# A decoder step on one core: two more idle products in the router, another order in the first pair of experts, and the sample rows first at the end

## The reference

```python
h = x + W_o( sigmoid(g_a) * Mamba2_SSD(n) + sigmoid(g_b) * ShortConv(n) )   # n = RMSNorm(x)
h = h + CrossAttn(RMSNorm(h), mem)                                         # 4 heads over 256 memory tokens
h = h + MoE(RMSNorm(h))
y = RMSNorm(h)

# MoE: 32 experts, top 4 of each token, softmax over the four logits
logits = x @ w_router + b_router;  top_v, top_i = top_k(logits, 4);  gates = softmax(top_v)
# one expert on the tokens that chose it
gu = xb @ w_gate_up[e] + b_gate_up[e];  gate, up = split(gu)
gate = min(gate, 7);  up = clip(up, -7, 7)
ys = ((up + 1) * gate * sigmoid(1.702 * gate)) @ w_down[e] + b_down[e]
out[token] += ys * gate_of_token
```

## Time and profile before

| | |
|---|---|
| median of 3 runs | 1407.49 us (1406.94 to 1408.96) |
| the profiled execution | 1408.71 us, of which the span from first to last instruction 1407.0 us |
| PE busy | 1374.1 us, 98% |
| DVE, ACT, POOL busy | 442.0, 218.2, 33.7 us |
| mean granted PE clock | 0.995 of full |
| moved by DMA | 497.24 MB; SP's queue 478.99 MB |

### The profile page before, as it was taken

One profiled execution on the slowest core, in us unless ns is written; L12 is line 12 of the kernel. 1 busy time (PEld: TensorE's weight loads), 2 busy tenths in 40 slices (PEclk: granted clock), 3 DMA queues, 4 the chain that ended last, 5 costly groups with the idle time before them and its releaser, 6 DMA issues.

```text
span 1407.0 us, 16092 instructions
## 1 busy us (share of the span) xinstructions
PE 1374.1 (98%) x6414; PEld 669.7 (48%) x6414; DVE 442.0 (31%) x905; ACT 218.2 (16%) x404; POOL 33.7 (2%) x60
## 2 busy tenths in 40 slices
PE   9999999999999999999999999999999999999997
PEld 7688887677756633333333333333333332333322
DVE  5634344862461412221211312213113121131213
ACT  2220022052123211100101111011011010110102
POOL 0000002200002000000000000000000000000000
PEclk9999999999999999999999999999999999999999
DMA  7644545975379899999999999999999999999995
GB/s 249 215 154 154 178 143 195 375 267 195 119 284 390 349 400 397 423 428 428 428 429 428 429 428 429 428 429 428 429 428 429 428 429 428 428 429 428 429 425 227
DMA packets 72119, 497.24 MB, mean 353 GB/s; under 512 B 8968, under 2 KB 10664, under 8 KB 47368
## 3 DMA queue, kind: packets, MB, share of 16 engines
q1 hardware_dynamic: 65852, 478.99, 82.8%
q0 software_dynamic: 4816, 15.54, 3.1%
q10 hardware_dynamic: 1412, 2.18, 0.5%
HBM read 488.61 MB, written 8.24 MB: 353 GB/s over the span
## 4 chain that ended last, share of the span: by engine, by line
PE 81%; DMA 15%; SPq 2%; DVE 1%; issue 1%; ACT 1%; DVEq 0%
PE bank L1504 77%; DMA wide<-in_w_gate_up 8%; DMA ring<-in_w_gate_up 6%; PE bank L1515 4%; DMA wdt<-in_w_in 1%; DVE wide L1427 1%; SPq L438 1%; SPq L441 0%; DVE wide L1487 0%; ACT wide L624 0%; ACT L634 0%; ACT L664 0%; ACT wide L615 0%; SPq L480 0%; SPq L428 0%
## 5 line engine op out<-in xcount | busy, mean ns | idle before, releaser
L1504 PE MATMUL bank<-ring,wide 128*64 128x512 f32 (+2 forms) x1696 | 403.3, 595 | 5.5 <-DMA ring<-in_w_gate_up 5.0
L1504 PE MATMUL bank<-wide 128*64 128x512 f32 (+6 forms) x1046 | 289.8, 575 | 11.4 <-DVE wide L1427 6.4
L1504 PE MATMUL bank<-tokT,ring 128*128 128x264 f32 x1152 | 264.1, 387 | 0.0
L1504 PEld LDWEIGHTS bank<-ring,wide 128*64 128x64 f32 (+2 forms) x1696 | 132.5, 140 | 258.1 <-issue 246.6
L1504 PEld LDWEIGHTS bank<-tokT,ring 128*128 128x128 f32 x1152 | 216.8, 190 | 41.1 <-issue 5.6
L1504 PEld LDWEIGHTS bank<-wide 128*64 128x64 f32 (+4 forms) x1046 | 98.4, 153 | 175.4 <-issue 122.7
L615 ACT ACTIVATE wide<-bank 64x512 f32<-64x512 f32 (+2 forms) x103 | 57.6, 560 | 339.0 <-PE bank L1504 218.5
L1451 DVE TENSOR_SCALAR wide<-bank 128x512 f32<-128x512 f32 x32 | 22.1, 692 | 274.1 <-PE bank L1504 274.1
L1504 PE MATMUL bank<-flat,wide 128*64 128x512 f32 (+2 forms) x408 | 92.9, 592 | 0.3 <-ACT wide L615 0.3
L1504 PE MATMUL bank<-conv,wide 128*64 128x512 f32 (+1 forms) x400 | 90.3, 593 | 0.0
L884 ACT ACTIVATE wide<-wide 128x512 f32<-128x512 f32 x32 | 20.2, 630 | 427.5 <-DVE wide L1451 427.5
(11 more groups left out here) (259 smaller groups left out, 737.8 us busy)
## 6 DMA issues: line engine op xcount, KB each, us to landing
ring<-in_w_gate_up SPq DMA_DIRECT2D x64, 2048.0 KB, 26.1
ring<-in_w_down SPq DMA_DIRECT2D x32, 2048.0 KB, 27.4
flat<-in_w_gate_up SPq DMA_DIRECT2D x16, 2048.0 KB, 24.5
conv<-in_w_gate_up SPq DMA_DIRECT2D x16, 2048.0 KB, 26.0
wide<-in_w_gate_up SPq DMA_DIRECT2D x16, 2048.0 KB, 27.4
tokT<-in_w_gate_up SPq DMA_DIRECT2D x16, 2048.0 KB, 25.1
ring<-in_w_in SPq DMA_DIRECT2D x15, 2048.0 KB, 12.4
wide<-in_w_down SPq DMA_DIRECT2D x8, 2048.0 KB, 25.6
```

The lines of the kernel that those rows point to most:

```text
L1504: last[0] = pe.matmul(out, lhsT, rhs, start=start, stop=stop)
```

## The change

1. Router: three `stay_warm` products of 512 columns take the place of one of 512 and one of 128. They stand ahead of `turn_tokens`, between the two experts' hidden biases, and behind `rank`. The products of `total` move from ahead of the first gather to between the two halves of `turn_rows`.
2. First pair: chunk 8 goes to ring place 8, chunk 9 to `acc` and `ytok`. So the refill of chunk 17 waits for stage 9 instead of 10, and ACT's first values of `acc` for stage 10 instead of 9. PE does `down` of the first expert right behind the eight `gate_up` stages; the gather stands behind stage 11, and `turn_rows` behind stage 12. ACT's `copy_rows` and DVE's `spread` move back with them. The other pairs keep their order.
3. End: sample rows first in `last_scatter`, in DVE's sums and in ACT's squares. Their root's reciprocal is DVE's, both multiplications and the store are POOL's. SP stores the prompt rows alone.

```diff
-        FIRST_SLOT = [0, 1, 2, 6, 3, 4, 5, 7, 9, 8, 0, 1]
+        FIRST_SLOT = [0, 1, 2, 6, 3, 4, 5, 7, 8, 9, 0, 1]
...
-            sp.dma_start(acc[:, :, :], moe_chunk(0, 8)[:, 0:3, :]).then_inc(moe_full[9], 16)
-            sp.dma_start(ytok, moe_chunk(0, 8)[:, 3, :]).then_inc(moe_full[9], 16)
+            sp.dma_start(acc[:, :, :], moe_chunk(0, 9)[:, 0:3, :]).then_inc(moe_full[9], 16)
+            sp.dma_start(ytok, moe_chunk(0, 9)[:, 3, :]).then_inc(moe_full[9], 16)
...
-            for g, done_stages in zip(range(AHEAD, AHEAD + 8), (1, 2, 3, 5, 6, 7, 8, 10)):
+            for g, done_stages in zip(range(AHEAD, AHEAD + 8), (1, 2, 3, 5, 6, 7, 8, 9)):
...
-            sp.wait_ge(S["y_ready"], 4)
-            sp.dma_start(outs[1].rearrange("b s n -> (b s) n"), acc[0:TS, 2, :]).then_inc(S["y_out"], 16)
-            sp.wait_ge(S["y_out"], 64)
+            sp.wait_ge(S["y_out"], 48)
...
+            pool.wait_ge(S["gfin_in"], 16)
+            pool.wait_ge(S["s_root"], 1)
+            st(pool.tensor_scalar(acc[0:TS, 2, :], acc[0:TS, 2, :], rfin[0:TS, 2:3], None, ALU.mult))
+            pool.tensor_tensor(out=acc[0:TS, 2, :], in0=acc[0:TS, 2, :], in1=gfin[0:TS, :], op=ALU.mult)\
+                .then_inc(S["s_ready"], 1)
+            pool.wait_ge(S["s_ready"], 1)
+            pool.dma_start(outs[1].rearrange("b s n -> (b s) n"), acc[0:TS, 2, :]).then_inc(S["s_out"], 16)
+            pool.wait_ge(S["s_out"], 16)
...
                 sigmoid(1)
-                if not final:
+                if not (first or final):
                     copy_rows(at(2, 3))
                 copy_turned(1)
                 if first:
-                    s.wait_ge(S["stage_done"], at(12, 9))
+                    s.wait_ge(S["stage_done"], at(12, 10))
...
                 copy_y(0)
+                if first:
+                    copy_rows(at(2, 3))
                 copy_y(1)
...
-            for i, t in enumerate((0, 1, 2)):
+            for i, t in enumerate((2, 0, 1)):
...
-                if not final:
+                if not (first or final):
                     spread(at(2, 2))
                 v.wait_ge(S["gt_full"], at(1, 1))
                 v.tensor_copy(gT, bank[4][:, 0:T]).then_inc(S["gT_ready"], 1)
+                if first:
+                    spread(at(2, 2))
...
+            accumulate(beyond(n), 0, True)
+            v.wait_ge(S["scat_read"], beyond(n)(5, -4))
+            v.memset(small[:, 310:311], 0.0).then_inc(S["tile_done"], 1)
+            accumulate(beyond(n), 1, True)
+            accumulate(beyond(n), 2, True)
+            v.wait_ge(S["scat_read"], beyond(n)(5, -2))
+            v.memset(small[:, 311:312], 0.0).then_inc(S["tile_done"], 1)
+            v.wait_ge(S["f_rms"], 1)
+            v.reciprocal(rfin[0:TS, 2:3], rfin[0:TS, 2:3]).then_inc(S["s_root"], 1)
+            accumulate(beyond(n), 3, True)
+            accumulate(beyond(n), 4, True)
+            v.wait_ge(S["scat_read"], beyond(n)(5, 0))
+            v.memset(small[:, 312:313], 0.0).then_inc(S["tile_done"], 1)
+            finish(1)
             finish(2)
...
             route(KB - 1)
+            stay_warm(bank[1], 512)
             turn_tokens(KB - 2)
             turn_tokens(KB - 1)
...
-            stay_warm(bank[1], 512)
-            for name, k in (("xo", 6), ("rs", 0), ("rt", 2), ("xtok", 3)):
+            for name, k in (("xo", 6), ("rs", 0)):
                 emptied(pe, name, k)
             pe.wait_ge(S["crossed_in"], 96)
-            hidden_bias(first_pair, 0)
+            hidden_bias(first_pair, 0, (0,))
+            emptied(pe, "rt", 2)
+            stay_warm(bank[7], 512)
+            emptied(pe, "xtok", 3)
+            hidden_bias(first_pair, 0, (1,))
...
+            stay_warm(bank[7], 512)
+            emptied(pe, "xtok", 5)
+            pe.wait_ge(S["xtok_ready"], 3)
+            gather(1)
+            turn_rows(1, (0,))
             b = free_bank(pe, "total")
...
-            stay_warm(bank[4], 128)
-            pe.wait_ge(S["xtok_ready"], 3)
-            gather(1)
-            turn_rows(1)
+            turn_rows(1, (1,))
...
+                elif first:
+                    output_bias(buf)
+                    down(0)
+                    turn_acts(1)
+                    turn_gates()
+                    down(1, (0,))
+                    pe.wait_ge(S["gT_ready"], at(1, 1))
+                    gather(at(1, 2))
+                    down(1, (1,))
+                    turn_rows(at(2, 3))
```

More of the change, by code:

```diff
@@ L1421, in accumulate @@
             def accumulate(at, j, last=False):
-                v.wait_ge(S["scat_full"], at(5, (j - 1) % 5 - 4 if last else j - 4))
+                v.wait_ge(S["scat_full"], at(5, j - 4))
                 if j == 0:
@@ L2009, in gather, with turn_rows @@
                     last[0].then_inc(S["xy_full"], 1)
-            def turn_rows(count):
-                for h in range(2):
+            def turn_rows(count, halves=(0, 1)):
+                for h in halves:
                     pe.wait_ge(S["xgt_ready"], count + h)
@@ L2037, in last_scatter @@
                 pe.wait_ge(S["gT_ready"], at(1, 0))
+                for h in range(2):
+                    mm(bank[5][32 * h:32 * h + TS, :], gT[:, TP:T], ytok[:, 512 * h:512 * h + 512])
+                last[0].then_inc(S["scat_full"], 1)
                 for t in range(2):
@@ L2041, in last_scatter, with hidden_bias @@
                         last[0].then_inc(S["scat_full"], 1)
-                for h in range(2):
-                    mm(bank[5][32 * h:32 * h + TS, :], gT[:, TP:T], ytok[:, 512 * h:512 * h + 512])
-                last[0].then_inc(S["scat_full"], 1)
-            def hidden_bias(at, buf):
+            def hidden_bias(at, buf, experts=(0, 1)):
                 pe.wait_ge(S["onehot_ready"], at(1, 1))
-                for e in range(2):
+                for e in experts:
                     for b in range(2):
@@ L2117, in turn_acts, with down @@
                     last[0].then_inc(S["turned"], 1)
-                def down(e):
+                def down(e, parts=(0, 1)):
                     pe.wait_ge(S["actT_ready"], at(2, e + 1))
-                    for part in range(2):
+                    for part in parts:
                         w = landed(8 + 2 * e + part)
@@ L2130, in down, with turn_gates @@
                         last[0].then_inc(S["stage_done"], 1)
+                def turn_gates():
+                    pe.wait_ge(S["selg_ready"], at(1, 1))
+                    for t, (c, r) in enumerate(TILES):
+                        turn(bank[4][:, c:c + r], selG[0:r, t, :])
+                    last[0].then_inc(S["gt_full"], 1)
                 if not first:
@@ L2159, in experts @@
                     pe.wait_ge(S["xg_ready"], at(2, 3))
-                pe.wait_ge(S["selg_ready"], at(1, 1))
-                for t, (c, r) in enumerate(TILES):
-                    turn(bank[4][:, c:c + r], selG[0:r, t, :])
-                last[0].then_inc(S["gt_full"], 1)
-                down(1)
+                    turn_gates()
+                    down(1)
             experts(first_pair, 0, 0, first=True)
```

22 lines of the change are left out of this document (8 added, 14 removed).

## The result

The changed kernel takes 1413.14 us (median of 9 runs, 1409.89 to 1415.26) against 1406.94 us for the kernel before, run beside it (9 runs, 1403.85 to 1408.96): ratio 1.0035, 95% interval 1.0022 to 1.0047. It is slower by 0.2 to 0.5%; the forecast said 1402.6 us, and its range ended at 1406.3. The profiled span is 1411.7 us against 1407.0.

A forecast was written before the change was run, and what follows sets the result against it. PE's pace bounds the kernel until 1007 us, then the weight stream. Router and first pair -4.8, end -0.7, sum -5.5: 1403.2 as profiled, 1402.0 from the median, middle taken 1402.6 us; range 1400.4 to 1406.3.

The forecast's parts named there:

- The end, forecast -0.7: Behind the last weights: samples first and POOL's share of the work end the span 0.7 us earlier, near SP's row.
- it ends between 1404.3 and 1410.0: End: POOL's two products, issue and store finish in this span of us, giving -0.9 to +3.0 against 1407.0.
- SP's path, forecast -0.9: End: SP's last prompt store issued at 1403.5 to 1403.7 instead of 1404.81, less 0.2 for its size: -0.9 us.
- Rival (3): End: POOL finishes at its upper bound, +3.0 instead of -0.7; all -1.8, 1406.3 us; chance 0.06.
- Rival (4): End: POOL's store sets it and takes 14.1 us; +10.1, with the -4.8 +5.3, 1413 us; chance 0.04.
- DVE's last multiplication: End: POOL's two-input product may block it, losing up to 1.4 us, +0.5 instead of -0.7; counted in the range only.
- I give back 0.2: End: allowance of 0.2 us because SP's last store is 256 KB instead of 32 KB.
- Router, forecast -2.7: Router: with the clock held, `gate_up` starts at 483.0 instead of 485.6; -2.7 us, bounds -3.2 and +0.5.
- rival (1): Router: the granted clock falls all the same; -1.7, with the end -2.4, 1405.7 us; chance 0.22.
- the idle product between the biases can hold `rank` by some tenths: Router: this delays `rank`, and so `select`, by some tenths of a us; gather taken to start at 476.5.
- First pair, forecast -2.1: First pair: earlier refill requests shrink the weight stream's hole from 4.7 to 2.6 us; -2.1 us.
- Later requests follow every 3.5 us, so no third hole appears: Weight stream behind the eleventh refill: requests come faster than the 4.90 us a chunk takes, so no further idle stretch.

The follow-up runs named there:

- e5: The kernel before with the new end alone, but SP issues the sample store and POOL still multiplies; ratio 1.0011 (0.9999 to 1.0023).
- e6: As e5, but POOL takes its two-input product with the gain first and the one-input scaling last; ratio to before 1.0001 (0.9990 to 1.0011).
- e1: The kernel before with the router's part of the change alone; ratio 1.0001 (0.9989 to 1.0014).
- e7: The kernel before with idle products where PE waits in the router, biases kept together, `total` between the transposes' halves; ratio 0.9987 (0.9974 to 0.9999).
- e2: The kernel before with the first pair's new order alone; ratio 0.9998 (0.9986 to 1.0010).
- e8: The kernel before with the first pair's new order in every pair but the last; ratio 0.9991 (0.9979 to 1.0003).
- e13: The kernel before, but POOL issues the sample store at the end and SP waits for it; ratio 1.0024 (1.0013 to 1.0035).
- e11: The kernel before, but POOL issues the sample store at the end and waits for it itself; ratio 1.0028 (1.0014 to 1.0042).

## Why the prediction was wrong

*The end, forecast -0.7, measured +4.2.* The step that failed was where POOL ends: "it ends between 1404.3 and 1410.0", made of two products, an issue and a store. Those terms were nearly sound. The products took 2.85 and 2.33 us (bounds 1.4 to 2.3 each, so one is over), the issue 0.60, the landing 2.9 (bounds 2.2 to 6.0), and POOL's wait was over at 1407.8, or 1407.3 in the time of before. That is 0.7 later than SP's wait was over before, within the range of -0.9 to +3.0. Missing was a term behind the last one: POOL's DRAIN of 3.50 us, which before lay at 461.76 us, where nothing waited for it. A second step failed beside it: SP's path, forecast -0.9, was 2.5 us late, for the reason in the next paragraph, so the end would have been late without the DRAIN too. e5 takes 2.6 us of the loss away by giving the store to SP, e6 another 1.5 by POOL's other order. "At the end nothing else loads the DMA engines" was also wrong, since SP's two halves are issued beside POOL's store, but the landing stayed within its bounds.

Rival (3), POOL late, had the right place and 3.0 us in place of 4.2; the chance of 0.06 was far too low. Rival (4) ends at 1413, the time that was measured, and that is luck: its store of 14.1 us took 2.9, and the 4.8 us that it took off for router and pair were not there.

*DVE's last multiplication, put "in the range only".* Here it happened: 3.58 us in place of 1.41, 2.2 more where the prediction had up to 1.4. e5 and e6 price it at 1.5 us where SP ends the kernel. The Trainium skill, "Advanced Engine Details and Errata", GPSIMD Details, says that the pool engine conflicts with DVE instructions that have two SBUF inputs. The trace agrees for POOL's two-input product (3.58, and 1.29 for sums with one operand from PSUM beside it); beside its one-input scaling DVE's 1024 columns took 1.29 us in the change and 1.63 in e6, with 1.28 before. The section that the prediction names puts its rule on DVE instructions in a two-port mode alone; the rule on two SBUF inputs is the one that fits this multiplication.

*SP's last store, forecast -0.9.* In the change it came at 1405.93, because DVE was held. Where DVE is not held the issue comes where it was put: in e6 SP's second half is issued by 1401.94, 17.2 us behind d, which is 1403.7 in the time of before. "I give back 0.2" for its size failed there: the stores now follow so closely that the DMA engines are nearly full to 1404, and nothing is left of the gain.

*Router, forecast -2.7, measured about 0.* Two steps failed. The clock fell all the same in the profiled execution, rival (1), whose chance was 0.22. And "the idle product between the biases can hold `rank` by some tenths" was 1.27 us: the idle product takes 1.06 us and the split biases about 0.9 more than together, and against that stood PE's wait of only 0.59. e1, where the clock held, shows the second alone: 1.33 us are left of the gain. e7 shows that the forecast's 2.6 us were there to be had, with the idle products elsewhere.

*First pair, forecast -2.1, measured about 0.* The requests came in the order and within 0.5 us of the distances worked out, and PE's new wait was 0.32 us, as forecast. But the new order costs PE more than that wait: in e2 the second pair starts 0.8 us later from l than before (91.97 against 91.14), where the prediction had 0.3. "Later requests follow every 3.5 us, so no third hole appears" failed: the second pair's gather holds request 28. Before, that request was issued at 581.68, with the 1.7 us that the prediction counts up to the transfer 583.4. The stream, done with the eleventh refill at 549.6 by the same working and with seven chunks more at 583.9, needed it then: it had 0.5 us to gain there, not 2.1, and in e2 that request comes 0.8 us later from l. e8 shows it from the other side: with the second pair's gather moved too, the third hole is gone. I followed the queue for four requests and took the rest from a rate.

*What bounds the kernel* held: PE's pace first, the stream later, with the last landing 0.47 us later, as the router's last product was 0.41 later in this execution.

## What to carry to other kernels

Before an engine that finished early is given the last instruction of a kernel, look at what it does when it closes, also in records that the busy rows leave out: here a DRAIN of 3.5 us became visible the moment the engine was last. Products that run side by side in different parts of the array are priced as a group; what was put between them here cost the group's time over again. A hole in a stream is closed only if every later request up to the point where the stream is continuous has the same lead, so follow the requests one by one through the next pair.

## What the runs showed of the hardware

POOL's closing DRAIN takes 3.42 to 3.50 us behind a wait, in every kernel here whose POOL ends with one, with or without a store of its own; without a wait it ends 3.44 to 3.50 us behind POOL's last work (e5, e6, e13). A 32 KB store by POOL lands 2.1 us after its issue behind SP's other stores (e11, e13) and 2.9 us beside SP's two halves (the change), against 1.8 us for SP's own before. A DVE multiplication with two SBUF operands waits for POOL's two-input product (2.92 us for the first half, 0.75 before). POOL needs 2.85 us for one-input scaling of 8x1024 and only 2.33 to 2.35 for the two-input product of the same size. Why the granted clock stayed down for longer in some executions than in others of the same router (`gate_up` 14.69 to 17.14 us behind the last logits product with the router of before) stays open.
